# Splitting a mixer tile into front, ssm_front, scan and back, and emitting the next tile's front between scan and back

## The chip, the cores and the metric

The kernel runs on 8 cores of one Trainium2 chip. Every core works on its own prompt sequence and its own 16 sample sequences; no data goes between cores. The metric is the device time of the slowest core, in microseconds (us).

## The reference

One layer of a hybrid decoder, applied to a prompt (8 x 2048 x 1024) and to samples (128 x 4 x 1024):

```python
n1 = _rmsnorm(x, g_mix); proj = n1 @ w_in                  # 1024 -> 1536
u, v, xs = split(proj, [512, 1024])
v = _rmsnorm(v per head, g_v)
a_out = u * (tril(w_s[h]) @ v + b_s)                       # in chunks of 128 positions
ys, hr, hi = _ssm_scan(xs, h0_re, h0_im, ...)              # 32 groups, complex diagonal state of 64
g = gelu(ys); b_out = g * sigmoid(g @ w_glu + b_glu)
mix = concat(_rmsnorm(a_out), _rmsnorm(b_out))
h = x + mix @ w_out                                        # the residual addition
up = _rmsnorm(h) @ w_ffn_in; conv = causal conv of width 3 over up
y = _rmsnorm(h + (gelu(gate) * val) @ w_ffn_out)
```

The states of the scan, the last rows of up and, for the samples, v are outputs too.

## The kernel before

A core runs setup (tables and weights for the scan, to about 288 us in the profile), then the mixer, which makes h, then the FFN, which reads h back from a tensor h1d in device memory. A barrier over all engines stands between them. The change is in the mixer alone.

**How the program is ordered.** The kernel builds a list of instructions for each engine in the order in which the Python code emits them (class Prog). A Buf object stands for each buffer and keeps its last writer and its readers; an instruction waits on semaphores for the last writer of what it reads, and for the last writer and the readers of what it writes. On an engine the instructions stand in emission order. The DMAs issued by SP (called "sp") form one list with SP's waits, and those issued by POOL (the Z gathers) stand in POOL's list. Nothing reorders by hand or by a planner.

**A mixer tile** (mixer_tile, called five times: four prompt tiles of 512 tokens, then one sample tile of 64) handles subtiles s = 0 to 3 of 128 tokens, the sample tile only one of 64. Its parts, in emission order:

- The x loads: four DMAs of 512 KB into xt, a buffer of four subtiles. For the sample tile, also 32 small DMAs of the old states into Hin (in R1 and R2's memory) and their transposes.
- a2(s) and a4(s): Square of x with a sum (ACT), root (ACT), reciprocal (DVE, L328), xn = x * rs * g_mix (DVE), eight transposes (PE), copy into n1T (ACT).
- stage1(s): 24 projection matmuls with w_in. stage1e(s): copies of u and xs out of the PSUM banks (ACT), the store of xs to a scratch tensor zscr, and the gather of it into Z with another layout, by a DMA that POOL issues.
- stage2(s): RMSNorm of v, matmul with Msg, and a_tm = (s + b_s) * u (DVE). stage2b(s): RMSNorm of a_tm into mixa (DVE), transposes, copy into mixT (ACT). It runs one subtile behind stage2.
- ssm_front, emitted after stage2(3) and before stage2b(2): transposes of Z into X2, copied out by ACT and DVE, matmuls with MinX, and sixteen products of DVE into R1, R2, mA and mB, which POOL sums.
- The scan: 64 tensor_tensor_scan instructions of DVE (L783), and products that give HPb and the carries C1 and C2, with mB from POOL.
- The rest: 64 matmuls with Toep and Mout, copies into Z (DVE and ACT in turn), transposes, gelu into gT (ACT), a cast of gT to gTb (DVE), the GLU matmuls, sigmoid and product into mixT, Square into sqb, and w_out: per subtile 16 matmuls into four banks and four DVE instructions that add to xt, then the store of xt to h1d.

PSUM banks are taken in turn, eight of them, by nb(). L254 and L257 are the helpers of matmul and transpose, L260 and L276 those of ACT, L263, L272 and L278 those of DVE, L281 that of the DMAs. The last loop of ffn_tile is a part that the prediction also looks at: per subtile it loads h1d into hb (three buffers), has 44 matmuls, adds them to hb on DVE, normalises and stores hb to yp:

```python
for si, (hrow, PT, oap, col0) in enumerate(subtiles):
    i3 = cnt["hb"] % 3; cnt["hb"] += 1
    dma("sp", hb[i3][0:PT, :], h1d[hrow:hrow + PT, :], [], [b_hb[i3]])
...
    dma("sp", oap, hb[i3][0:PT, :], [b_hb[i3]], [], is_output=True)
```

Of the kernel before, what the change touches and what calls it, by code (L numbers as in the profile page):

```python
# [207 lines left out]
def build_nc():  # L208
# [28 lines left out]
    zscr = nc.dram_tensor("zscr", [2112, 512], BF16).ap()  # L237

    ES = contextlib.ExitStack()
    with ES:  # L240
# [267 lines left out]
        with contextlib.ExitStack() as SA:  # L508
# [21 lines left out]
            xt = sba("xt", [128, 4, 1024]); b_xts = [Buf() for _ in range(4)]  # L530
# [14 lines left out]
            mixT = sba("mixT", [128, 8, 512], BF16); b_mixT = Buf()  # L545
# [7 lines left out]
            gT = sba("gT", [128, 4, 512]); b_gT = Buf()  # L553
# [3 lines left out]
            bT = gT; b_bT = b_gT  # L557
# [36 lines left out]
            def mixer_tile(tok0, src, ntok, sample, h1row):  # L594
# [3 lines left out]
                if sample:  # L598
                    dma("sp", xt[0:64, 0, :], src, [], [b_xts[0]])
                else:  # L600
                    for s_ in range(4):
                        dma("sp", xt[:, s_, :], src[tok0 + 128 * s_:tok0 + 128 * (s_ + 1), :], [], [b_xts[s_]])
                if sample:
                    bk1, bbk1 = nb(); bk2, bbk2 = nb()
                    for gq in range(8):
                        gs = slice(gq * 4, gq * 4 + 4)
                        Hin = Hins[gq % 2]; b_Hin = b_Hins[gq % 2]
                        dma("sp", Hin[:, :, 0:64], sre[:, gs, :], [], [b_Hin]); dma("sp", Hin[:, :, 64:128], sim[:, gs, :], [], [b_Hin])
                        dma("sp", Hin[:, :, 128:192], sim[:, gs, :], [], [b_Hin]); dma("sp", Hin[:, :, 192:256], sre[:, gs, :], [], [b_Hin])
                        for gl in range(4):  # L610
                            g = gq * 4 + gl
                            tr(bk1[:, g * 16:(g + 1) * 16], Hin[:, gl, 0:128], identf[0:16, 0:16], [b_Hin, b_identf], [bbk1])
                            tr(bk2[:, g * 16:(g + 1) * 16], Hin[:, gl, 128:256], identf[0:16, 0:16], [b_Hin, b_identf], [bbk2])
                    f2 = lambda v_: v_.rearrange("p g b -> p (g b)")
                    cp("act", f2(V10), bk1[:, 0:512], [bbk1], [b_V10])
                    cp("dve", f2(V20), bk2[:, 0:512], [bbk2], [b_V20])
                    cp("dve", HPb[:, :, 0:16], V10, [b_V10], [b_HPb])
                    shb = [128, 32, 16]
                    tt("dve", Vend, V10, AR4[:].unsqueeze(2).broadcast_to(shb), ALU.mult, [b_V10, b_A4], [b_Vend])
                    tt("dve", Vt, V20, AI4[:].unsqueeze(2).broadcast_to(shb), ALU.mult, [b_V20, b_A4], [b_Vt])  # L620
                    tt("dve", Vend, Vend, Vt, ALU.add, [b_Vend, b_Vt], [b_Vend])

                b_ss_s = [Buf() for _ in range(4)]; b_rs_s = [Buf() for _ in range(4)]; b_tm_s = [Buf() for _ in range(4)]
                b_n1T_s = b_n1T_list

                def a2(s):
                    act(junk[0:PT, :], xt[0:PT, s, :], AF.Square, [b_xts[s]], [b_junk, b_ss_s[s]], accum_out=ss4[0:PT, s:s + 1])
                    rstd(rs4[0:PT, s:s + 1], ss4[0:PT, s:s + 1], 1024.0, PT, 1, [b_ss_s[s]], [b_rs_s[s]], tm4[0:PT, s:s + 1], b_tm_s[s])

                def a4(s):  # L630
                    k2 = s % 2
                    stt(xn[k2][0:PT, :], xt[0:PT, s, :], rs4[0:PT, s:s + 1], gmix_bc[0:PT, :], ALU.mult, ALU.mult,
                        [b_xts[s], b_rs_s[s], b_gmix], [b_xn[k2]])
                    bk, bb = nb()
                    bkb = bk[:].bitcast(BF16)
                    for dti in range(8):
                        tr(bkb[:, dti * PT:(dti + 1) * PT], xn[k2][0:PT, dti * 128:(dti + 1) * 128], identb[0:PT, 0:PT],
                           [b_xn[k2], b_identb], [bb])
                    cp("act", n1T[:, :, s * 128:s * 128 + PT], bkb[:, 0:8 * PT].rearrange("p (a t) -> p a t", a=8), [bb], [b_n1T_s[s]])
# [19 lines left out]
                def stage1e(s, bu, bbu, bx, bbx):
                    k2 = s % 2  # L660
                    cp("act", u_tm[k2][0:PT, :], bu[0:PT, :], [bbu], [b_u[k2]])
                    cp("act", xs_tm[0:PT, s, :], bx[0:PT, :], [bbx], [b_xs_s[s]])
                    b_zs = Buf()
                    if sample:
                        dma("sp", zscr[2048:2112, :], xs_tm[0:64, 0, :], [b_xs_s[0]], [b_zs])
                        zv = zscr[2048:2112, :].rearrange("(b t) c -> b t c", t=4)
                        dma("pool", Z[0:16, 0:4, :], zv, [b_zs], [b_Z_s[0]])
                        dma("pool", Z[0:16, 4:8, :], zv, [b_zs], [b_Z_s[0]])
                    else:
                        r0 = h1row + 128 * s  # L670
                        dma("sp", zscr[r0:r0 + 128, :], xs_tm[:, s, :], [b_xs_s[s]], [b_zs])
                        dma("pool", Z[16 * s:16 * s + 16, :, :], zscr[r0:r0 + 128, :].rearrange("(k i) c -> k i c", i=8), [b_zs], [b_Z_s[s]])

                def stage2(s, bv, bbv):
                    k2 = s % 2
                    tsl = slice(s * 128, s * 128 + PT)
                    act(vsq[0:PT, :], bv[0:PT, :], AF.Square, [bbv], [b_vsq])
                    P.op("dve", lambda e: e.reduce_sum(out=ssv[0:PT, :], in_=vsq[0:PT, :].rearrange("p (h d) -> p h d", h=4), axis=AX.X),
                         [b_vsq], [b_ssv])
                    rstd(rv[0:PT, :], ssv[0:PT, :], 128.0, PT, 4, [b_ssv], [b_rv], tmv[0:PT, :], b_tmv)  # L680
                    tt("dve", vtmp[0:PT, :].rearrange("p (h d) -> p h d", h=4), bv[0:PT, :].rearrange("p (h d) -> p h d", h=4),
                       rv[0:PT, :].unsqueeze(2).broadcast_to([PT, 4, 128]), ALU.mult, [bbv, b_rv], [b_vtmp])
                    if sample:
                        tt("dve", vnf[0:PT, :], vtmp[0:PT, :], gv_bc[0:PT, :], ALU.mult, [b_vtmp, b_gv], [b_vnf])
                        dma("sp", vs, vnf[0:PT, :], [b_vnf], [], is_output=True)
                        cp("dve", vn[k2][0:PT, :], vnf[0:PT, :], [b_vnf], [b_vn[k2]])
                    else:
                        tt("dve", vn[k2][0:PT, :], vtmp[0:PT, :], gv_bc[0:PT, :], ALU.mult, [b_vtmp, b_gv], [b_vn[k2]])
                    bs_, bbs = nb()
                    for h in range(4):  # L690
                        lhs = Msg_s[:, h, :] if sample else Msg[:, h, :]
                        mm(bs_[0:PT, h * 128:(h + 1) * 128], lhs, vn[k2][0:PT, h * 128:(h + 1) * 128], True, True,
                           [b_Msg, b_vn[k2]], [bbs])
                    bsb = bsT_s if sample else bsT
                    a_tm = a_tms[k2]; b_atm = b_atms[k2]
                    for h in range(4):
                        stt(a_tm[0:PT, h * 128:(h + 1) * 128], bs_[0:PT, h * 128:(h + 1) * 128], bsb[0:PT, h:h + 1],
                            u_tm[k2][0:PT, h * 128:(h + 1) * 128], ALU.add, ALU.mult, [bbs, b_col, b_u[k2]], [b_atm])
# [51 lines left out]
                for s in range(NS):  # L750
                    nxt = stage1(s + 1) if s + 1 < NS else None
                    stage2(s, pend[0], pend[1])
                    if s == NS - 1:
                        b1, bb1 = ssm_front()
# [372 lines left out]
```

How the kernel before makes its waits and increments, by code:

```python
            def run(ename, eng):  # L158
                waited = {}
                for o in self.ops[ename]:
                    for d in o.deps:
                        if d.kind == "c":
                            key = ("c", d.eng)
                            val = d.seq
                            sem = esem[d.eng]
                        else:
                            key = ("d", d.eng, d.dsem)
                            val = d.dval
                            sem = dsem[d.eng][d.dsem]
                        if waited.get(key, 0) >= val:
                            continue
                        waited[key] = val
                        eng.wait_ge(sem, val)
                    ins = o.emit(eng)
                    if o.kind == "c":
                        if o.marked:
                            ins.then_inc(esem[ename], 1)
                    else:
                        ins.then_inc(dsem[ename][o.dsem], 16)
                fin = {}
                for o in self.out_dmas:
                    if o.eng == ename:
                        fin[o.dsem] = max(fin.get(o.dsem, 0), o.dval)
                for s, v in fin.items():
                    eng.wait_ge(dsem[ename][s], v)
```

## Time and profile before

| | us |
|---|---|
| runs shown | 1723.48 and 1761.52, median 1742.5 |
| the profiled execution, its own time | 1719.03 |
| its span, on the profiled core (5) | 1717.5 |
| spans of the eight cores in it | 1706.6 to 1717.5 |
| PE, DVE, ACT, POOL busy | 858.1, 902.4, 552.9, 305.7 |

The profile shows one execution on its slowest core. Busy times are sums over the span. A row of the timeline gives the start of an instruction (or of a run of like ones), its length, engine, line, kind, what it writes and reads, how many, and in brackets how long the engine was idle before it and who released it. Times of rows are counted from the span's start.

### The profile page before, as it was taken

The numbers are of one execution on the slowest core, as the hardware profiler recorded it, in microseconds if no ns is written. First come the engines' busy times: TensorE is split into PE (matmuls) and PEld (weight loads), VectorE is DVE, ScalarE is ACT, GpSimd is POOL, SyncE is SP. The second block draws the span as 40 slices with busy tenths as digits, with TensorE's granted clock in tenths as the row PEclk, the third lists the DMA queues.
The fourth block names the chain that finished last, engine by engine and source line by source line (L and its number), as shares of the span: only waits on it lengthen the run. The fifth ranks groups of instructions, "written<-read, shape, count | busy, mean of one in ns | idle before, by whom it ended". The sixth has DMA issues, their size and how long they took to land.

```text
span 1717.5 us, 18591 instructions; the slowest of 8 cores (1706.6 to 1717.5 us)
## 1 busy us (share of the span) xinstructions
PE 858.1 (50%) x4925; PEld 440.4 (26%) x4925; DVE 902.4 (53%) x1638; ACT 552.9 (32%) x1359; POOL 305.7 (18%) x319
## 2 busy tenths in 40 slices
PE   0002100615542561553242525877869378888696
PEld 0002100313221231322122313333324133334243
DVE  0388720484356348436531204899942258888522
ACT  0200101313322230332210306565631277676411
POOL 1000002030021003002100010555530014444200
PEclk9997555857765785776575656999989779999898
DMA  5600001000200200020010063777753435555033
GB/s 75 83 6 0 2 25 57 22 4 22 86 16 1 98 22 4 26 83 16 1 60 8 15 110 95 80 91 86 82 75 99 132 70 56 53 54 55 7 115 99
DMA packets 138807, 89.70 MB, mean 52 GB/s; under 512 B 115943, under 2 KB 122159, under 8 KB 138447
## 3 DMA queue, kind: packets, MB, share of 16 engines
q0 software_dynamic: 99136, 36.84, 19.0%
q1 hardware_dynamic: 39567, 51.67, 9.6%
q8 instruction: 41, 0.67, 0.2%
q14 instruction: 63, 0.52, 0.1%
HBM read 102.45 MB, written 20.64 MB: 72 GB/s over the span
## 4 chain that ended last, share of the span: by engine, by line
DVE 25%; DMA 24%; PE 19%; issue 14%; ACT 13%; POOL 3%; SPq 1%; DVEq 1%; ACTq 0%; POOLq 0%
PE bank L254 15%; DMA wst<-w_ffn_in 6%; DMA hb<-h1d 4%; DVE acc L272 4%; PE bank L257 3%; DVE R L783 3%; ACT acc L260 2%; ACT junkB L260 2%; DMA w_in_sb<-w_in 2%; POOL zt L263 2%; DMA R<-sim 2%; DMA R<-w_s 1%; DVE hb L263 1%; DVE hb L272 1%; DMA xt<-xp 1%
## 5 line engine op out<-in xcount | busy, mean ns | idle before, releaser
L254 PE MATMUL bank<-n2T,wst 128*128 128x512 bf16 (+1 forms) x1760 | 345.2, 357 | 64.4 <-ACT acc L260 25.4
L254 PEld LDWEIGHTS bank<-n2T,wst 128*128 128x128 bf16 x1760 | 154.6, 101 | 254.8 <-issue 106.2
L272 DVE SCALAR_TENSOR_TENSOR acc<-upS,cw,acc 128x512 f32<-128x512 f32 (+1 forms) x264 | 178.3, 688 | 30.6 <-ACT hsv L276 15.5
L260 ACT ACTIVATE acc<-bank,cw 128x512 f32<-128x512 f32 (+1 forms) x220 | 156.0, 709 | 111.2 <-POOL zt L263 111.2
L254 PE MATMUL bank<-wfo,zt 128*128 128x512 bf16 (+1 forms) x748 | 166.0, 386 | 25.2 <-POOL zt L263 25.2
L263 POOL TENSOR_TENSOR zt<-acc,acc 128x512 bf16<-128x512 f32 (+1 forms) x110 | 122.5, 1114 | 207.5 <-ACT cst_s L276 118.1
L272 DVE SCALAR_TENSOR_TENSOR acc<-bank,cw,acc 128x511 f32<-128x511 f32 (+1 forms) x176 | 131.2, 746 | 10.8 <-ACT upS L276 1.3
L281 POOL DMA_DIRECT2D wst<-w_ffn_in x88 | 79.7, 906 | 190.5 <-DMA wst<-w_ffn_in 180.0
L254 PEld LDWEIGHTS bank<-wfo,zt 128*128 128x128 bf16 (+1 forms) x748 | 74.5, 100 | 116.3 <-issue 31.6
L254 PE MATMUL bank<-w_in_sb,n1T 128*128 128x512 bf16 (+1 forms) x408 | 98.2, 402 | 0.8 <-ACT n1T L276 0.8
L281 POOL DMA_DIRECT2D Z<-zscr x18 | 9.0, 503 | 491.4 <-DMA zscr<-xs_tm 489.1
L257 PE MATMUL bank<-identf,R 16*128 16x16 f32 (+3 forms) x104 | 15.4, 299 | 155.8 <-DMA R<-w_s 111.4
L260 ACT ACTIVATE junkB<-hb 128x1024 bf16<-128x1024 f32 (+1 forms) x34 | 35.7, 1051 | 167.5 <-DVE hb L263 159.6
L272 DVE SCALAR_TENSOR_TENSOR acc<-hsv,cw,acc 128x1 f32<-128x1 f32 (+1 forms) x176 | 75.1, 426 | 19.7 <-DVE acc L272 1.8
L263 DVE TENSOR_TENSOR hb<-hb,bank 128x512 f32<-128x512 f32 (+1 forms) x34 | 23.4, 688 | 108.1 <-DMA hb<-h1d 80.7
L254 PE MATMUL bank<-Mout,HPb 128*64 128x128 bf16 (+1 forms) x160 | 30.5, 270 | 92.7 <-DVE C L263 92.7
L254 PE MATMUL bank<-w_out_sb,mixT 128*128 128x512 bf16 (+1 forms) x272 | 68.6, 419 | 0.0
L260 ACT ACTIVATE acc<-acc 128x512 f32<-128x512 f32 (+1 forms) x110 | 61.2, 556 | 14.3 <-DVE acc L272 14.2
L276 ACT ACTIVATE upS<-bank 128x512 f32<-128x512 f32 (+1 forms) x132 | 62.3, 472 | 9.6 <-PE bank L254 9.5
L260 ACT ACTIVATE gTb<-xt 128x1024 bf16<-128x1024 f32 (+1 forms) x17 | 17.9, 1050 | 124.8 <-DMA xt<-xp 124.8
L257 PE MATMUL bank<-identb,xn 128*128 128x128 bf16 (+1 forms) x136 | 16.8, 302 | 82.3 <-DVE xn L272 82.3
L254 PEld LDWEIGHTS bank<-w_in_sb,n1T 128*128 128x128 bf16 (+1 forms) x408 | 42.1, 105 | 51.6 <-issue 11.3
(220 smaller groups left out, 1276.7 us busy)
## 6 DMA issues: line engine op xcount, KB each, us to landing
wst<-w_ffn_in POOLq DMA_DIRECT2D x88, 256.0 KB, 4.5
hb<-h1d SPq DMA_DIRECT2D x32, 512.0 KB
xt<-xp SPq DMA_DIRECT2D x16, 512.0 KB
h1d<-xt SPq DMA_DIRECT2D x16, 512.0 KB
yp<-hb SPq DMA_DIRECT2D x16, 512.0 KB
wfo<-w_ffn_out POOLq DMA_DIRECT2D x22, 256.0 KB, 4.8
w_in_sb<-w_in POOLq DMA_DIRECT2D x8, 256.0 KB, 4.5
w_out_sb<-w_out POOLq DMA_DIRECT2D x8, 256.0 KB, 4.0
```

Of the source, the lines that this page charges most:

```text
L254: P.op("pe", lambda e: e.matmul(out, lhsT, rhs, start=start, stop=stop), reads, writes)
L257: P.op("pe", lambda e: e.transpose(out, in_, ident), reads, writes)
L260: P.op("act", lambda e: e.activation(out=out, in_=in_, func=func, **kw), reads, writes)
L263: P.op(eng, lambda e: e.tensor_tensor(out=out, in0=in0, in1=in1, op=op), reads, writes)
L272: P.op("dve", lambda e: e.scalar_tensor_tensor(out=out, in0=in0, scalar=scalar, in1=in1, op0=op0, op1=op1), reads, writes)
L276: P.op(eng, lambda e: e.activation(out=out, in_=in_, func=AF.Copy), reads, writes)
L281: P.dma(q, lambda e: e.dma_start(out=out, in_=in_, **kw), reads, writes, is_output=is_output)
L783: P.op("dve", lambda e, RR=RR, g=g: e.tensor_tensor_scan(out=RR[:, g, :], data0=MG8[:, g:g + 1].broadcast_to([128, 64]), data1=RR[:, g, :] ...
```

## The change

mixer_tile no longer runs a tile but returns four functions, and the caller emits them in a new order:

```python
tiles[0][0]()
tiles[0][1]()
for t in range(5):
    tiles[t][2]()
    if t + 1 < 5:
        tiles[t + 1][0]()
    tiles[t][3]()
...
    if t + 1 < 5:
        tiles[t + 1][1]()
```

[0] is front (x loads, a2, a4, stage1, stage1e, stage2, stage2b), [1] is ssm_front (now with the Z gathers, and for the sample tile with the loads of the old states), [2] is scan, [3] is back. The outputs of the prompt's last state are emitted after back(3). With that go these edits:

- xt with four subtiles becomes xa, two buffers of one subtile each for the front, and xh, two buffers of one subtile each for back. back loads x again from device memory into xh.
- The x load of subtile s is emitted in a2(s), and not four at once.
- The gather of Z is emitted in ssm_front. All zscr stores and Z gathers go by one Buf, b_zscr, where each store had one of its own.
- mixT is split into mixTa (two buffers, by the tile's parity) and mixTb.
- gT and its cast to bf16 are gone; gelu writes gTb.

```diff
-            xt = sba("xt", [128, 4, 1024]); b_xts = [Buf() for _ in range(4)]
+            xa = [sba("xa%d" % i, [128, 1024]) for i in range(2)]; b_xa = [Buf(), Buf()]
+            xh = [sba("xh%d" % i, [128, 1024]) for i in range(2)]; b_xh = [Buf(), Buf()]
...
+                    def a2(s):
+                        xs_ = xa[s % 2]; bxs_ = b_xa[s % 2]
+                        if sample:
+                            dma("sp", xs_[0:64, :], src, [], [bxs_])
+                        else:
+                            dma("sp", xs_[:, :], src[tok0 + 128 * s:tok0 + 128 * (s + 1), :], [], [bxs_])
+                        act(junk[0:PT, :], xs_[0:PT, :], AF.Square, [bxs_], [b_junk, b_ss_s[s]], accum_out=ss4[0:PT, s:s + 1])
...
+                    a2(0)
+                    for s in range(NS):
+                        if s + 1 < NS:
+                            a2(s + 1)
+                        a4(s)
...
+                    pend = stage1(0)
+                    stage1e(0, *pend[2:])
+                    lag = None
+                    for s in range(NS):
+                        nxt = stage1(s + 1) if s + 1 < NS else None
+                        stage2(s, pend[0], pend[1])
+                        if lag is not None:
+                            stage2b(lag)
+                        if nxt is not None:
+                            stage1e(s + 1, *nxt[2:])
+                        lag = s
+                        pend = nxt
+                    stage2b(lag)
...
+                        for s_ in range(4):
+                            r0 = h1row + 128 * s_
+                            dma("pool", Z[16 * s_:16 * s_ + 16, :, :], zscr[r0:r0 + 128, :].rearrange("(k i) c -> k i c", i=8), [b_zscr], [b_Zs[s_]])
...
+                            act(gTb[:, cb, 0:ntok].rearrange("p (k j) -> p j k", j=NJ),
+                                bkb[:, o0:o0 + NJ * NC].rearrange("p (j k) -> p j k", j=NJ), AF.Gelu_apprx_tanh, [bb], [b_gTb])
...
-                cp("dve", gTb[:, :, 0:ntok], gT[:, :, 0:ntok], [b_gT], [b_gTb])
...
+                    for s in range(NS):
+                        tsl = slice(s * 128, s * 128 + PT)
+                        hi_ = cnt_a["xh"] % 2; cnt_a["xh"] += 1
+                        xh_ = xh[hi_]; bxh_ = b_xh[hi_]
+                        if sample:
+                            dma("sp", xh_[0:64, :], src, [], [bxh_])
+                        else:
+                            dma("sp", xh_[:, :], src[tok0 + 128 * s:tok0 + 128 * (s + 1), :], [], [bxh_])
...
+                            xsl = xh_[0:PT, nh * 512:(nh + 1) * 512]
+                            tt("dve", xsl, xsl, bka[0:PT, :], ALU.add, [bxh_, bba], [bxh_])
+                            stt(xsl, bkb_[0:PT, :], rb4[0:PT, s:s + 1], xsl, ALU.mult, ALU.add, [bxh_, bbb, b_rb4], [bxh_])
+                        if sample:
+                            dma("sp", h1d[h1row:h1row + 64, :], xh_[0:64, :], [bxh_], [])
+                        else:
+                            dma("sp", h1d[h1row + 128 * s:h1row + 128 * (s + 1), :], xh_[:, :], [bxh_], [])
```

## Rows read from the trace of the kernel before

**Rows 1.** The profile's page, its head.

```profile
span 1717.5 us, 18591 instructions; the slowest of 8 cores (1706.6 to 1717.5 us)
```

**Rows 2.** Busy time by stretch: start and end, length, each engine, PEclk, DMA share, GB/s.

```profile
587.80:610.00 22.20, 3.79 (x32) 3.11 (x33) 5.70 (x8) 8.43 (x15) 0.00 (x0) 0.51 0.34 117
...
666.00:690.00 24.00, 0.83 (x5) 0.48 (x5) 22.72 (x90) 0.83 (x2) 5.04 (x4) 0.50 0.00 0
```

**Rows 3.** Timeline (columns as told above) of the start of tile 2.

```profile
586.11 0.75 DVE L272 SCALAR_TENSOR_TENSOR xt<-bank,rb,xt 128x512 f32<-128x512 f32 x1 [0.17 <-PE bank L254]
...
587.76 2.99 SPq L281 DMA_DIRECT2D xt<-xp  x4
...
592.16 1.06 ACT L260 ACTIVATE gTb<-xt 128x1024 bf16<-128x1024 f32 x1 [20.82 <-DMA xt<-xp]
...
593.79 0.16 DVE L328 RECIPROCAL rs<-tm 128x1 f32<-128x1 f32 x1 [6.93 <-ACT tm L260]
...
596.04 1.28 DVE L272 SCALAR_TENSOR_TENSOR xn<-xt,rs,gmix_bc 128x1024 bf16<-128x1024 f32 x1
...
606.62 2.48 DVE L272 SCALAR_TENSOR_TENSOR xn<-xt,rs,gmix_bc 128x1024 bf16<-128x1024 f32 x2
...
610.05 11.50 PE L254 MATMUL bank<-w_in_sb,n1T 128*128 128x512 bf16 x48
```

**Rows 4.** Timeline, the start of tile 0.

```profile
288.26 1.77 SPq L281 DMA_DIRECT2D xt<-xp  x4
...
291.97 1.06 ACT L260 ACTIVATE gTb<-xt 128x1024 bf16<-128x1024 f32 x1 [62.62 <-DMA xt<-xp]
```

**Rows 5.** Timeline of tile 2, from stage2(3) to the first Mout matmul.

```profile
646.11 1.71 DVE L272 SCALAR_TENSOR_TENSOR a_tm<-bank,bsT,u_tm 128x128 f32<-128x128 f32 x4 [0.84 <-PE bank L254]
...
649.54 0.69 DVE L278 COPY X<-bank 128x1024 bf16<-128x1024 bf16 x1 [1.72 <-ACT X L276]
...
661.46 0.77 DVE L272 SCALAR_TENSOR_TENSOR mixa<-a_tm,ra,goa_bc 128x512 bf16<-128x512 f32 x1
...
661.64 1.71 POOL L263 TENSOR_TENSOR R<-R,mB 128x512 f32<-128x512 f32 x1
...
666.04 0.58 PE L257 MATMUL bank<-identb,mixa 128*128 128x128 bf16 x4 [3.08 <-DVE cA L263]
...
666.63 5.56 DVE L783 TENSOR_TENSOR_SCAN R<-MG,R 128x64 f32<-128x64 f32 x24
...
690.04 0.28 PE L254 MATMUL bank<-Mout,HPb 128*64 128x128 bf16 x1 [23.18 <-DVE C L263]
```

**Rows 6.** Timeline of tile 2, gelu to GLU.

```profile
704.22 1.23 DVE L278 CAST gTb<-gT 128x2048 bf16<-128x2048 f32 x1 [7.66 <-ACT gT L260]
...
705.59 6.28 PE L254 MATMUL bank<-gTb,w_glu_sb 128*128 128x512 bf16 x16 [7.00 <-DVE gTb L278]
```

**Rows 7.** Timeline of tile 2, DVE's additions of w_out.

```profile
720.15 0.69 DVE L263 TENSOR_TENSOR xt<-xt,bank 128x512 f32<-128x512 f32 x1 [0.28 <-issue]
...
724.09 0.69 DVE L263 TENSOR_TENSOR xt<-xt,bank 128x512 f32<-128x512 f32 x1
...
733.64 0.75 DVE L272 SCALAR_TENSOR_TENSOR xt<-bank,rb,xt 128x512 f32<-128x512 f32 x1 [0.17 <-PE bank L254]
```

**Rows 8.** The FFN's h1d loads: who waited for them (us, times), then timeline rows.

```profile
  DVE hb L263: 80.7, 15
...
1291.10 0.69 DVE L263 TENSOR_TENSOR hb<-hb,bank 128x512 f32<-128x512 f32 x1 [7.13 <-DMA hb<-h1d]
...
1641.61 0.33 SPq L281 DMA_DIRECT2D hb<-h1d  x1
...
1645.68 0.69 DVE L263 TENSOR_TENSOR hb<-hb,bank 128x512 f32<-128x512 f32 x1 [4.63 <-DMA hb<-h1d]
```

**Rows 9.** Timeline of the sample tile, DVE and PE.

```profile
935.66 1.28 DVE L272 SCALAR_TENSOR_TENSOR xn<-xt,rs,gmix_bc 64x1024 bf16<-64x1024 f32 x1
...
959.49 5.64 PE L257 MATMUL bank<-identf,R 128*16 128x128 f32 x32 [0.54 <-ACT mixT L276]
```

More of the change, by code:

```diff
@@ L237, in build_nc @@
     zscr = nc.dram_tensor("zscr", [2112, 512], BF16).ap()
+    b_zscr = Buf()
     ES = contextlib.ExitStack()
@@ L597, in mixer_tile @@
                 NC = 16 if sample else 64
[L598 to L639, printed above, removed]
@@ L659, in stage1e @@
[L659 to L663, printed above, removed]
-                    if sample:
-                        dma("sp", zscr[2048:2112, :], xs_tm[0:64, 0, :], [b_xs_s[0]], [b_zs])
+                mixTa_t = mixTa[par]; b_mixTa_t = b_mixTa[par]
+                shared = {}
@@ L674, in stage2 @@
[L674 to L698, printed above, removed]
@@ L744, in ssm_front @@
                             tt("pool", R2[:, gs, :], R2[:, gs, :], mB[:], ALU.subtract, wr2 + [b_mB], wr2)
-                    return (b1, bb1) if sample else (None, None)
-                pend = stage1(0)
-                stage1e(0, *pend[2:])
-                lag = None
[L750 to L754, printed above, removed]
-                    if lag is not None:
-                        stage2b(lag)
-                    if nxt is not None:
-                        stage1e(s + 1, *nxt[2:])
-                    lag = s
-                    pend = nxt
@@ L765, in mixer_tile, with back @@
+                def back():
+                    Zy = Z
                     for gq in range(8):
@@ L829, in mixer_tile @@
-                act(sqb[:, :, 0:ntok], mixT[:, 4:8, 0:ntok], AF.Square, [b_mixT], [b_sqb, b_R1[8]])
-                bkR, bbR = nb()
-                for s in range(NS):
-                    tsl = slice(s * 128, s * 128 + PT)
-                    for m in range(4):
-                        mm(bkR[0:PT, s:s + 1], sqb[:, m, tsl], onesb[:, 0:1], m == 0, m == 3, [b_ones, b_sqb, b_R1[8]], [bbR])
-                rstd(rb4[0:PT, 0:NS], bkR[0:PT, 0:NS], 512.0, PT, NS, [bbR], [b_rb4], tb4[0:PT, 0:NS], b_tb4)
@@ L849, in mixer_tile @@
-                if sample:
-                    dma("sp", h1d[h1row:h1row + 64, :], xt[0:64, 0, :], [b_xts[0]], [])
-            for t in range(4):
-                mixer_tile(512 * t, xp, 512, False, 512 * t)
-            bk, bb = nb()
-            tr(bk[0:32, 0:128], C1[:], identf[:], [b_C, b_identf], [bb])
-            cp("act", stS[:], bk[0:32, 0:128], [bb], [b_stS])
-            dma("sp", srep, stS[:, 0:64], [b_stS], [], is_output=True)
-            dma("sp", simp, stS[:, 64:128], [b_stS], [], is_output=True)
@@ L859, in build_nc @@
-            mixer_tile(0, xs, 64, True, 2048)
+                            if sample:
+                                mm(bk[0:NC, gl * 128:(gl + 1) * 128], X2[0:64, g, 0:NC], Toep[0:64, g, :], True, False, [b_X2, b_Toep], [bb])
+                            else:
+                                mm(bk[0:NC, gl * 128:(gl + 1) * 128], X2[:, g, 0:NC], Toep[:, g, :], True, False, [b_X2, b_Toep], [bb])
+                            mm(bk[0:NC, gl * 128:(gl + 1) * 128], HPb[:, g, 0:NC], Mout[:, g, :], False, True, [b_HPb, b_Mout], [bb])
@@ new lines, in back @@
+                        cp("dve" if gq % 2 == 0 else "act", Zy[0:NC, :, 64 * gq:64 * gq + 64].rearrange("p j (g c) -> p g j c", g=4),
+                           bk[0:NC, 0:512].rearrange("p (g j c) -> p g j c", g=4, j=8), [bb], b_Zs)
+                    NJ = 4 if sample else 8
+                    for cbp in range(2):
+                        bk, bb = nb()
+                        bkb = bk[:].bitcast(BF16)
+                        for cl in range(2):
+                            cb = cbp * 2 + cl
+                            for j in range(NJ):
+                                o0 = (cl * NJ + j) * NC
+                                tr(bkb[:, o0:o0 + NC], Zy[0:NC, j, cb * 128:(cb + 1) * 128], identb[0:NC, 0:NC], b_Zs + [b_identb], [bb])
+                        for cl in range(2):
+                            cb = cbp * 2 + cl
+                            o0 = cl * NJ * NC
+                            act(gTb[:, cb, 0:ntok].rearrange("p (k j) -> p j k", j=NJ),
+                                bkb[:, o0:o0 + NJ * NC].rearrange("p (j k) -> p j k", j=NJ), AF.Gelu_apprx_tanh, [bb], [b_gTb])
@@ new lines, in back @@
+                    for m in range(4):
+                        bk, bb = nb()
+                        for kt in range(4):
+                            mm(bk[:, 0:ntok], w_glu_sb[:, kt, m * 128:(m + 1) * 128], gTb[:, kt, 0:ntok], kt == 0, kt == 3, [b_wglu, b_gTb], [bb])
+                        act(sg[:, 0:ntok], bk[:, 0:ntok], AF.Sigmoid, [bb, b_col], [b_sg], bias=bglu[:, m:m + 1])
+                        tt("dve", mixTb[:, m, 0:ntok], gTb[:, m, 0:ntok], sg[:, 0:ntok], ALU.mult, [b_gTb, b_sg], [b_mixTb])
@@ new lines, in back @@
+                    act(sqb[:, :, 0:ntok], mixTb[:, :, 0:ntok], AF.Square, [b_mixTb], [b_sqb, b_R1[8]])
+                    bkR, bbR = nb()
+                    for s in range(NS):
+                        tsl = slice(s * 128, s * 128 + PT)
+                        for m in range(4):
+                            mm(bkR[0:PT, s:s + 1], sqb[:, m, tsl], onesb[:, 0:1], m == 0, m == 3, [b_ones, b_sqb, b_R1[8]], [bbR])
+                    rstd(rb4[0:PT, 0:NS], bkR[0:PT, 0:NS], 512.0, PT, NS, [bbR], [b_rb4], tb4[0:PT, 0:NS], b_tb4)
@@ new lines, in mixer_tile @@
+                return front, ssm_front, scan, back
+            tiles = [mixer_tile(512 * t, xp, 512, False, 512 * t, t % 2) for t in range(4)]
+            tiles.append(mixer_tile(0, xs, 64, True, 2048, 0))
+            tiles[0][0]()
[5 more added lines that the diff above has]
+                tiles[t][3]()
+                if t == 3:
+                    bk, bb = nb()
+                    tr(bk[0:32, 0:128], C1[:], identf[:], [b_C, b_identf], [bb])
+                    cp("act", stS[:], bk[0:32, 0:128], [bb], [b_stS])
+                    dma("sp", srep, stS[:, 0:64], [b_stS], [], is_output=True)
+                    dma("sp", simp, stS[:, 64:128], [b_stS], [], is_output=True)
+                if t + 1 < 5:
+                    tiles[t + 1][1]()
```

252 lines of the change are left out of this document (140 added, 112 removed).

## The prediction

> **What bounds the kernel now.** I read the page first: the profiled core spans 1717.5 us [rows 1], and outside that span the execution's own time of 1719.0 us has 1.5 us. The part that is changed, the mixer, runs from the first x load at 288.3 us [rows 4] to the barrier ahead of the FFN. No engine is full there, so I cut one prompt tile (tile 2) into stretches and looked in each for the wait that ends last. Three things stand out.
>
> At the tile's start everything stands still for x. DVE ends the previous tile's last addition at 586.86, SP issues the four x loads at 587.76, ACT gets the first at 592.16, and the first projection matmul runs at 610.05, 23.2 us after DVE's last work [rows 3]. Most of that is not the load: it is a ring Square, reciprocal, xn, transposes, copy, repeated for each subtile, with PE busy 3.79 us of 22.2 [rows 2].
>
> In the scan DVE is busy 22.72 of 24 us and PE 0.83 [rows 2]; PE's first Mout matmul has then waited 23.18 us for DVE [rows 5]. So the scan is DVE's, and the scan is the bound there.
>
> Last, w_out: PE and DVE alternate, 3.94 us for subtile 0 and (734.39 - 724.09) / 3 = 3.43 us for each of the others [rows 7]. x is in SBUF then, nothing waits for a DMA.
>
> **The change part by part.** The emission order becomes scan(t), front(t+1), back(t), ssm_front(t+1). Each engine still runs its own list in order. The row of mixa(2) shows it: DVE ran it at 661.46 with no idle time before it, straight after the sixteen products that stand ahead of it in the list [rows 5]. So what counts is what each engine has ahead of the moved work.
>
> *Front under the scan.* Every subtile of the front needs DVE (reciprocal and xn) before PE can transpose. These stand behind scan(t) on DVE. Only the loads, Squares and roots of subtiles 0 and 1 can run under the scan, on SP and ACT. PE's idle 23 us stay.
>
> *The x ring.* xt held four subtiles, xa holds two. Loads 0 and 1 of tile t+1 stand on SP behind back(t-1)'s last store and land under ssm_front(t) and scan(t): hidden. Load 2 needs xa[0], read by xn(0), which DVE runs after scan(t); load 3 needs xa[1], read by xn(1), which stands behind reciprocal 2, which needs load 2. Both loads are exposed, one after the other. A load issued into a quiet queue took 291.97 - 288.26 = 3.7 us until ACT ran [rows 4]; Square to reciprocal is 593.79 - 592.16 = 1.6; xn is 1.3 (half of 2.48); from xn(2)'s start to the first matmul 610.05 - 606.62 = 3.4 [rows 3]. From scan end: reciprocals and xn(0) 1.7, load 3.7, Square path 1.6, reciprocal and xn(1) 1.5, load 3.7, Square path 1.6, reciprocal 0.2, 3.4: 17.4, with 0.1 for each of some six handovers 18.0 us. Before it was 23.2. Saved 5.2 for tiles 1 to 3: -15.6. Tile 0 has no earlier work to hide under: xn(0) to matmul was 610.05 - 596.04 = 14.0 [rows 3], becomes 18.0 - 0.4 = 17.6: +3.6.
>
> *Stage 2 to scan.* ssm_front stood between stage2(3) and stage2b(2), so that products and mixa shared the time: a_tm ended at 647.8 (four of 1.71 us in all from 646.11) and the scan began at 666.63, 18.8 us [rows 5]. Now both stage2b come first: from mixa(2) (661.46) to the end of PE's transposes of mixa(3) (666.04 + 0.58) is 5.2, with 0.4 for the reciprocal 5.6 us, and PE turns to back(t). ssm_front then stands alone, from the X copy (649.54) to POOL's last sum (661.64 + 1.71 = 663.35) and 0.6 for the carries: 14.4 us [rows 5]. 5.6 + 14.4 = 20.0 against 18.8: +1.2 for each of four tiles, +4.8. The Z gathers move on POOL's queue from the front to ssm_front. They need back(t)'s transposes of Z, done before the GLU, and POOL has nothing else; w_out covers them at no cost, otherwise one gather after another of a few us would be late, then the X transposes. The shared b_zscr chains the zscr stores; SP waits there, but xh load 0 behind it is wanted only 30 us later.
>
> *gT goes.* The cast of 1.23 us and its handovers go: PE began the GLU 705.59 - 704.22 = 1.4 us after the cast's start [rows 6]; -1.4 each, -5.5 for four tiles.
>
> *The residual is loaded again.* back loads x a second time. In SP's list this is load(s), store(s), load(s+1), store(s+1). Store(s) waits for DVE's last addition of s, and load(s+1) stands behind it, although xh has another buffer that is free. So load(s+1) is issued when DVE has run dry, and DVE waits for all of it; 3 per tile, 12 in all (load 0 and the sample's lie ahead of other work). Behind DVE's waiting addition stand the rest of back and all of ssm_front(t+1): its X copy is a DVE instruction, so the scan is late by the same. The kernel has the same pattern with the same 512 KB in its FFN: hb load behind the yp store. There DVE waited 80.7 us over 15 times, 5.4 each; from 4.63 (a load issued at 1641.61) to 7.13 [rows 8]. I take the mean. The additions, now free of PE, run 0.1 faster than 3.43. 12 x (5.4 - 0.1) = +63.6.
>
> *Sample tile.* Its front goes from between the state loads and the state output (935.66 to 959.49 [rows 9]) to between scan(3) and back(3). About as long in either place, and nothing runs beside it in either: I cost this at 0, bounds -3 and +3. The state loads keep their chain.
>
> Sum: 3.6 - 15.6 + 4.8 - 5.5 + 63.6 = +50.9. 1719.0 + 50.9 = 1770 us. The two runs shown are 1723.5 and 1761.5, median 1742.5; the profiled execution is 0.3% under the lower one, and my time is to be held against executions like it. A median like theirs would stand some 20 us higher.
>
> Of the load's price: the rows say 3.9 to 7.1 us for 512 KB. The Trainium skill, DMA: Bandwidth & Descriptors, section on the anatomy of one DMA, gives about 2.0 us fixed plus bytes over bandwidth (for DMAs issued from GpSimd), and its Bandwidth section about 358 GB/s per core where both cores of a pair stream; an estimate by that page is 3.5 us, and the sum with it would be near 1756. The trace's loads are longer than that page's figure, so it is not used.
>
> **The rivals.**
>
> *The second load is covered (the other side, not slower).* Were the 12 loads to land under DVE's additions, the sum would be 50.9 - 63.6 = -12.7, 1706 us. It turns where a load costs 12.7 / 12 = 1.1 us; a result within 2% of before needs less than (34.4 + 12.7) / 12 = 3.9. For it: two xh buffers, and PE, done ahead by two subtiles, never waits. Against: SP's order, and the 15 waits of hb, which has three buffers and waits nevertheless. Chance 0.08. The Trainium skill, same page, Rules for kernel authors, says to issue a DMA early, compute, and wait late, since the fixed cost then overlaps. By that rule this would be the result, if the issue were early; the rows of hb show what a store ahead in the queue makes of it.
>
> *The change does what its name says.* The front truly runs under the scan: 3 x 18.0 us less than my sum, 1716 us. For it: PE and ACT are free. Against: xn is DVE's. Chance 0.03.
>
> *The stores get in the way.* Each xh load runs beside the store issued 0.5 us earlier, as hb's do. At the dearest wait, 7.13, the sum is 12 x 1.7 = 21 higher, 1791; if loads 2 and 3 of x also take the 4.4 us of the first load of tile 2, issued behind a store (592.16 - 587.76 [rows 3]), in place of 3.7, it is 8 x 0.7 = 6 more: 1797. Chance 0.17.
>
> *Cheap end.* Every load at 4.63: 12 x 0.8 = 9 less, 1761; with 3 us from the sample tile, and 0.6 per tile if PE, fresh from the front, ran the first four GLU matmuls at the pace of w_in's (11.50 / 48 = 0.24 [rows 3] against 6.28 / 16 = 0.39 [rows 6]), 1756. Chance 0.2, and the forecast itself 0.52.
>
> **How the numbers follow.** The range 1750 to 1806 takes in the forecast, the cheap end and the store case, with 6 to 9 us beyond for what I rounded and, above, for a median that like the one shown lies over the profiled execution; left out are the first two rivals, 0.11, and the tails. About 2%, 34 us, is what a measurement can tell from no change; slower by over that begins at 1753 in this accounting. The forecast, the cheap end (nearly all) and the dear end lie past it: 0.76. Within 2%: the two first rivals and the rest of the cheap end, 0.2. Faster by over 2% needs the front hidden and the loads hidden: 0.04.
>
> **What would show it.** Right: DVE waits for xh<-x some 5 us twelve times, each behind an h1d store; the gap of PE before the first Mout matmul stays; ACT waits for x twice per tile, about 3 us, after xn(0) and xn(1); a steady tile lasts 147.5 - 5.2 + 1.2 - 1.4 + 15.9 = 158 us, where 147.5 is the distance between DVE's last additions of two tiles, 586.86 and 734.39 [rows 3, 7]. Wrong: xh waits under 2 us; or PE transposes xn during the scan. The weakest term is the price of one exposed load; 1 us there is 12 us in the sum.

## The result and the profile after

| | before | changed | 
|---|---|---|
| median of all runs, us | 1729.6 (10 runs) | 1793.0 (11 runs) |
| the profiled execution, us | 1719.0 | 1784.2 |

The changed kernel is slower: the ratio of its time to that of before is 1.0366, with a 95% interval of 1.0335 to 1.0396. The forecast was 1770, made against 1719; the profiled executions differ by 65.1 us where the sum had 50.9. Some executions of every kernel fall into a slower state with a lower TensorE clock: the medians here are of all executions and the ratios of the others alone, and of the profiles used below only that of the old order with the new buffers shows such an execution. The page of the changed kernel begins:

```profile
span 1782.6 us, 18661 instructions; the slowest of 8 cores (1772.1 to 1782.6 us)
...
PE 863.9 (48%) x4925; PEld 439.9 (25%) x4925; DVE 902.5 (51%) x1633; ACT 575.5 (32%) x1359; POOL 303.3 (17%) x319
...
DVE  0398711483256426432822011688982238888632
```

DVE's busy time has not moved (902.5 against 902.4), PE's has grown by 6 us and ACT's by 22.6 (575.5 against 552.9), the span [rows 1] by 65. Over the whole span no engine is full: most of the 65 us is time in which engines wait for one another, and the third point below shows what ACT's 22.6 us are.

The first thing to look at is the start of tile 2, the timeline of the same stretch as [rows 3], DVE first, then ACT and PE (start, length, what, and in brackets the idle time before and its releaser; the helpers' lines stand one lower than in the kernel before, L261 for L260, L273 for L272 and so on):

```profile
559.52 0.17 DVE L264 TENSOR_TENSOR C<-cA,cB 128x8 f32<-128x8 f32 x1
...
559.89 1.28 DVE L273 SCALAR_TENSOR_TENSOR xn<-xa,rs,gmix_bc 128x1024 bf16<-128x1024 f32 x1
...
566.58 0.16 DVE L329 RECIPROCAL rs<-tm 128x1 f32<-128x1 f32 x1 [5.40 <-ACT tm L261]
...
564.94 1.06 ACT L261 ACTIVATE gTb<-xa 128x1024 bf16<-128x1024 f32 x1 [1.48 <-DMA xa<-xp]
...
571.95 1.06 ACT L261 ACTIVATE gTb<-xa 128x1024 bf16<-128x1024 f32 x1 [1.64 <-DMA xa<-xp]
...
561.32 1.01 PE L258 MATMUL bank<-identb,xn 128*128 128x128 bf16 x8 [34.94 <-DVE xn L273]
...
577.26 11.71 PE L255 MATMUL bank<-w_in_sb,n1T 128*128 128x512 bf16 x48
```

The scan ends at 559.69, and xn(0) follows with no gap: loads 0 and 1 are hidden. ACT waits for loads 2 and 3, DVE for ACT, and w_in's matmuls begin 17.6 us after the scan's end, where it was 23.2 after DVE's last addition. PE has waited 34.94 us for xn: nothing of the front was under the scan except what SP and ACT had of it.

Second, the additions of w_out, SP's list and DVE's (compare [rows 7, 8]), and then, from the view of the tile xh, what the instructions that write it waited for in the whole execution (us, times):

```profile
661.32 0.32 SPq L282 DMA_DIRECT2D h1d<-xh  x1
...
661.78 0.33 SPq L282 DMA_DIRECT2D xh<-xp  x1
...
665.84 0.69 DVE L264 TENSOR_TENSOR xh<-xh,bank 128x512 f32<-128x512 f32 x1 [4.60 <-DMA xh<-xp]
...
675.55 0.69 DVE L264 TENSOR_TENSOR xh<-xh,bank 128x512 f32<-128x512 f32 x1 [6.32 <-DMA xh<-xp]
...
687.22 0.68 DVE L279 COPY X<-bank 128x1024 bf16<-128x1024 bf16 x1
```

```profile
  DMA xh<-xp: 55.0, 11
```

Store, load, wait, as in the FFN. Eleven waits are put down to the load, 5.0 us each, and the additions of a tile take 29.9 us (657.38 to 687.30) in place of 14.2. The X copy of the next ssm_front stands right behind them at 687.22. The prediction had twelve such waits.

Third, what was not forecast, gelu and the GLU's first matmul (compare [rows 6]), first in the kernel before and then in the changed one:

```profile
699.50 4.62 ACT L260 ACTIVATE gT<-bank 128x512 f32<-128x512 bf16 x4
```

```profile
632.75 10.00 ACT L261 ACTIVATE gTb<-bank 128x512 bf16<-128x512 bf16 x4
...
643.00 6.02 PE L255 MATMUL bank<-gTb,w_glu_sb 128*128 128x512 bf16 x16 [10.78 <-ACT gTb L261]
```

The four gelu instructions of a tile take 10.0 us; in the kernel before they took 4.6. PE waits 10.78 us for them, where it waited 7.00 for gelu and the cast [rows 6].

### The profile page after: what moved, and what is told of

Same layout as the page of the kernel before. It is cut to its first block, busy times and chain, and to the rows that moved or that the text cites. A ratio compares the mean times of both kernels' runs of the same rounds, so it can differ in the third digit from the quotient of the medians.

```text
span 1782.6 us, 18661 instructions; the slowest of 8 cores (1772.1 to 1782.6 us)
## 1 busy us (share of the span) xinstructions
PE 863.9 (48%) x4925; PEld 439.9 (25%) x4925; DVE 902.5 (51%) x1633; ACT 575.5 (32%) x1359; POOL 303.3 (17%) x319
## 4 chain that ended last, share of the span: by engine, by line
DVE 28%; DMA 24%; PE 16%; ACT 13%; issue 13%; POOL 3%; SPq 1%; DVEq 1%; ACTq 0%; POOLq 0%
PE bank L255 14%; DMA wst<-w_ffn_in 6%; DVE acc L273 5%; DMA hb<-h1d 4%; ACT gTb L261 3%; DVE R L793 3%; DMA xh<-xp 2%; PE bank L258 2%; ACT acc L261 2%; DMA xa<-xp 2%; ACT junkB L261 2%; DMA w_in_sb<-w_in 2%; POOL zt L264 2%; DMA R<-sim 1%; DVE hb L264 1%
## 5 line engine op out<-in xcount | busy, mean ns | idle before, releaser
L273 DVE SCALAR_TENSOR_TENSOR acc<-upS,cw,acc 128x512 f32<-128x512 f32 (+1 forms) x264 | 178.9, 691 | 36.8 <-ACT hsv L277 22.1
L261 ACT ACTIVATE acc<-bank,cw 128x512 f32<-128x512 f32 (+1 forms) x220 | 155.9, 709 | 113.2 <-POOL zt L264 113.2
L273 DVE SCALAR_TENSOR_TENSOR acc<-bank,cw,acc 128x511 f32<-128x511 f32 (+1 forms) x176 | 131.2, 745 | 10.7 <-ACT upS L277 1.6
L258 PE MATMUL bank<-identb,xn 128*128 128x128 bf16 (+1 forms) x136 | 16.8, 301 | 194.9 <-DVE xn L273 194.9
L255 PE MATMUL bank<-w_in_sb,n1T 128*128 128x512 bf16 (+1 forms) x408 | 102.6, 415 | 0.8 <-ACT n1T L277 0.8
L261 ACT ACTIVATE junkB<-hb 128x1024 bf16<-128x1024 f32 (+1 forms) x34 | 35.8, 1052 | 161.3 <-DVE hb L264 152.5
L273 DVE SCALAR_TENSOR_TENSOR acc<-hsv,cw,acc 128x1 f32<-128x1 f32 (+1 forms) x176 | 76.7, 436 | 18.3
L277 ACT ACTIVATE n1T<-bank 128x1024 bf16<-128x1024 bf16 (+1 forms) x17 | 17.0, 998 | 160.1 <-PE bank L258 160.1
L261 ACT ACTIVATE acc<-acc 128x512 f32<-128x512 f32 (+1 forms) x110 | 61.2, 556 | 13.0 <-DVE acc L273 12.9
L258 PEld LDWEIGHTS bank<-identb,xn 128*128 128x128 bf16 (+1 forms) x136 | 12.8, 136 | 198.4 <-issue 198.4
L264 DVE TENSOR_TENSOR xh<-xh,bank 128x512 f32<-128x512 f32 (+1 forms) x34 | 23.4, 687 | 67.3 <-DMA xh<-xp 55.0
L264 DVE TENSOR_TENSOR mixTb<-gTb,sg 128x512 bf16<-128x512 bf16 (+1 forms) x20 | 12.0, 599 | 89.7 <-ACT sg L261 89.7
```

Source lines behind the costliest of these rows:

```text
L255: P.op("pe", lambda e: e.matmul(out, lhsT, rhs, start=start, stop=stop), reads, writes)
L258: P.op("pe", lambda e: e.transpose(out, in_, ident), reads, writes)
L261: P.op("act", lambda e: e.activation(out=out, in_=in_, func=func, **kw), reads, writes)
L264: P.op(eng, lambda e: e.tensor_tensor(out=out, in0=in0, in1=in1, op=op), reads, writes)
L273: P.op("dve", lambda e: e.scalar_tensor_tensor(out=out, in0=in0, scalar=scalar, in1=in1, op0=op0, op1=op1), reads, writes)
L277: P.op(eng, lambda e: e.activation(out=out, in_=in_, func=AF.Copy), reads, writes)
```

## The experiments

All times are medians; the kernel before stood at 1728.6 to 1730.1 beside them. The changed kernel was not run again beside them: its time is the 1793.0 of the result above.

**Gelu to f32 again.** The changed kernel, with gelu's output in R2's memory, which is free in back:

```diff
+            gT = R2[:].rearrange("p g k -> p (g k)").rearrange("p (a t) -> p a t", a=4)
...
-                            act(gTb[:, cb, 0:ntok].rearrange("p (k j) -> p j k", j=NJ),
+                            act(gT[:, cb, 0:ntok].rearrange("p (k j) -> p j k", j=NJ),
...
+                    cp("dve", gTb[:, :, 0:ntok], gT[:, :, 0:ntok], b_R2, [b_gTb])
```

> The changed kernel with gelu written to f32 again (into R2's memory, which is free in back) and cast to bf16, as in the kernel before; all else as changed. Theory A, the strided bf16 output is what makes gelu slow (four of them 10.0 us in the changed kernel, 4.6 before): gelu falls to 4.6 us, from the table load to the first GLU matmul it is 7.4 us again in place of 11.6, and the time falls by 4 x 4.2 = 17 us, to 1776 from a median of 1793. Rival B, gelu is slow for another reason that came with the new order (what ran before it, the banks, the power state): gelu stays at 10 us, the cast comes on top, +5 us, 1798.

Measured: 1773.1, ratio to before 1.0245 (1.0207 to 1.0283), 20 us under the changed kernel. The groups of gelu by form, of the kernel before, the changed kernel and this one (busy us in all, mean ns of one; idle time before):

```profile
L260 ACT ACTIVATE gT<-bank 128x512 f32<-128x512 bf16 x16 | 17.4, 1085 | 1.4 <-ACT gT L260 0.4
```

```profile
L261 ACT ACTIVATE gTb<-bank 128x512 bf16<-128x512 bf16 x16 | 38.9, 2431 | 1.1
```

```profile
L261 ACT ACTIVATE R<-bank 128x512 f32<-128x512 bf16 x16 | 17.4, 1085 | 1.1
```

2431 ns become 1085 again, the kernel before's own figure, with all else in the new order. Theory A, that gelu's output is the cause, holds (it expected 1776).

**The same edit alone, in the kernel before.**

```diff
-                        act(gT[:, cb, 0:ntok].rearrange("p (k j) -> p j k", j=NJ),
+                        act(gTb[:, cb, 0:ntok].rearrange("p (k j) -> p j k", j=NJ),
...
-                cp("dve", gTb[:, :, 0:ntok], gT[:, :, 0:ntok], [b_gT], [b_gTb])
```

> The kernel before with one edit of the change alone: gelu writes bf16 straight into gTb and the cast is gone. Theory A, strided bf16 output is slow in any place: gelu 10 us in place of 4.6, less the cast, +4.2 per prompt tile, +17, 1747 from 1730. Rival B, as the prediction had it: the cast's 1.4 us go and nothing else changes, -5.5, 1724.

Measured: 1741.4, ratio 1.0071 (1.0052 to 1.0089). The same group by form:

```profile
L260 ACT ACTIVATE gTb<-bank 128x512 bf16<-128x512 bf16 x16 | 38.9, 2432 | 1.4 <-ACT gTb L260 0.4
```

2432 ns in the old order too. The edit costs 13 us by the medians and 19 by the profiled executions (1737.9 against 1719.0), on either side of the 17 expected; a step that I had counted as a gain is a loss in both orders.

**Gelu in plain order.** The changed kernel, with the two rearranges of gelu gone:

```diff
-                            act(gTb[:, cb, 0:ntok].rearrange("p (k j) -> p j k", j=NJ),
-                                bkb[:, o0:o0 + NJ * NC].rearrange("p (j k) -> p j k", j=NJ), AF.Gelu_apprx_tanh, [bb], [b_gTb])
+                            act(gTb[:, cb, 0:ntok],
+                                bkb[:, o0:o0 + NJ * NC], AF.Gelu_apprx_tanh, [bb], [b_gTb])
```

> The changed kernel with gelu reading its bank and writing gTb in plain order, both contiguous, still bf16; this leaves out the reordering of tokens, so y is another. Theory A, the slow gelu comes of writing two-byte values at a stride of eight: contiguous, one takes 0.6 to 1.1 us in place of 2.43, and the time is 20 us or more under the changed kernel. Rival B, it comes of bf16 output from this bank as such: 2.4 us as before the edit, no gain.

Measured once: 1756.6, 36 us under the changed kernel. The same group:

```profile
L261 ACT ACTIVATE gTb<-bank 128x512 bf16<-128x512 bf16 x16 | 9.6, 597 | 1.1
```

597 ns. So bf16 as such is not slow. The input was read in the same order in all of them; what differs is the output's step: none, 597 ns; eight f32 elements (32 bytes), 1085; eight bf16 elements (16 bytes), 2431. The Trainium skill, SBUF — State Buffer, in its note on cachelines in the section on the DMA port swizzle, says that SBUF has lines of 16 bytes and that each access to a new line costs extra. Both strided outputs take a new line for each element, so the rule agrees with both being slower than 597, but it doesn't say why 16-byte steps of bf16 are 2.2 times as dear as 32-byte steps of f32.

The sample tile's gelu is a second case, with a step of four elements in place of eight. From the same views, the changed kernel, the kernel before and this one:

```profile
L261 ACT ACTIVATE gTb<-bank 128x64 bf16<-128x64 bf16 x4 | 1.2, 310 | 0.3
```

```profile
L260 ACT ACTIVATE gT<-bank 128x64 f32<-128x64 bf16 x4 | 1.1, 282 | 0.3
```

```profile
L261 ACT ACTIVATE gTb<-bank 128x64 bf16<-128x64 bf16 x4 | 0.9, 224 | 0.3
```

Here the strided bf16 output is only 1.1 times as dear as the f32 one (310 against 282 ns; contiguous 224). So the price of a strided bf16 output depends on the step and not on the type alone, and lines of 16 bytes don't account for it: at this step bf16 has two elements to a line and f32 one, and bf16 is still the dearer. The cause stays open.

**The residual loads early.** Four xh buffers don't fit into SBUF, the on-chip memory, beside the rest (gTb then needs 4096 bytes per partition where 3200 are left). So in the changed kernel subtiles 0 and 3 go into xh, 1 and 2 into R2's memory, and no load stands behind a store:

```diff
+                    xhs = [(xh[0], [b_xh[0]]), (R2v[:, 0:1024], b_R2[0:16]), (R2v[:, 1024:2048], b_R2[16:32]), (xh[1], [b_xh[1]])]
...
+                    xload(0)
+                    if not sample:
+                        xload(3)
                     for gq in range(8):
...
+                    if not sample:
+                        xload(1)
+                        xload(2)
                     act(sqb[:, :, 0:ntok], mixTb[:, :, 0:ntok], AF.Square, [b_mixTb], [b_sqb, b_R1[8]])
...
-                        hi_ = cnt_a["xh"] % 2; cnt_a["xh"] += 1
-                        xh_ = xh[hi_]; bxh_ = b_xh[hi_]
+                        xh_, bxh_ = xhs[s]
```

> The changed kernel with the four residual loads of a tile issued early: the first and last subtile into xh at the start of back, the two in the middle into R2's memory (free in back) after the GLU; no load stands behind a store any more. Theory A, the exposed residual loads are the main loss: the 11 waits of DVE for xh in the profiled execution (55 us) and a twelfth go, and the time falls by 55 to 60 from a median of 1793, to 1735. By the runs so far the two repairs together gave 1717 and gelu alone 20 of it, so 1736 again. Rival B, the two losses overlapped in part, and each repair alone gives more than its share: 1728 or less, or the loads alone give less, 1745 or more.

Measured: 1737.3, ratio 1.0047 (1.0028 to 1.0067), 56 us under the changed kernel. SP's list in tile 2, and then what the instructions that write xh still wait for:

```profile
597.80 0.88 SPq L282 DMA_DIRECT2D xh<-xp  x2
...
598.88 1.49 SPq L282 DMA_DIRECT2D R<-xp  x2
...
647.92 0.33 SPq L282 DMA_DIRECT2D h1d<-xh  x1
```

```profile
  PE bank L255: 11.7, 24
```

The loads go out 49 us ahead of the first store; no wait for xh<-xp or for R<-xp is left, only PE's pace. 56 is the whole of the 55.0 that DVE had waited.

**Both repairs.** The edits of gelu to f32 and of the early loads together, in the changed kernel. While gelu uses R2's memory, the two residual loads that go there wait until the product with the GLU's gate has read it.

> The two repairs together, f32 gelu with cast (its own run: 1773) and early residual loads; the new order stays. Theory A, the two losses lie one behind the other on the same chain and add: 1793 - 20 - 57 = 1716, 0.7% under before (1729), which is what the hidden x loads of the new order are worth less the longer way to the scan (-12.7 in the prediction's sum). Rival B, the order is worth more once nothing hides it: 1700 or less. Rival C, it costs: over before, 1735 or more. In this kernel gelu's output and two of the loads share R2, so loads 1 and 2 are issued only some 5 us ahead of the additions; up to 2 us a tile may be exposed.

Measured: 1716.6, ratio 0.9917 (0.9888 to 0.9945). The two losses add (20 + 56 = 76, measured 1793.0 - 1716.6 = 76.4). With them gone, the rest of the change is 13 us faster than the kernel before (1730.1 beside it). The prediction's terms without the loads and without gelu come to 3.6 - 15.6 + 4.8 = -7.2; the profiled executions, by which the sum was made, give -7.4 (1711.66 against 1719.03), and the medians -13.4. Where the 6 us between the two come from isn't shown: the profiled execution of the kernel before is faster than each of its executions beside this one (1726.6 to 1738.0).

**The old order, with the new buffers.** The loop at the end of the mixer:

```diff
                 tiles[t][2]()
-                if t + 1 < 5:
-                    tiles[t + 1][0]()
                 tiles[t][3]()
...
                 if t + 1 < 5:
+                    tiles[t + 1][0]()
                     tiles[t + 1][1]()
```

> The changed kernel with the emission order undone (scan, back, then front and ssm_front of the next tile), all buffers as changed. Theory A, the new order is worth the x loads 0 and 1 and their Squares, nothing more: without it from scan or back to the first projection matmul about 26.4 us in place of 17.6, 3 x 8.8 for the prompt tiles and some 4 for the sample tile, +30, 1823. Rival B, the new order is worth nothing or costs (front ahead of back delays back and no engine gains): 1793 or less. Rival C, the front did hide behind more than that: 1850 or more.

Measured: 1820.1, ratio 1.0510 (1.0469 to 1.0551), 27 us over the changed kernel. So the new order of the tiles by itself brings 27 us, and what comes with it (the buffers, gelu's output, ssm_front behind stage2b) costs 90: 76 are the two losses, and the other 14 were not taken apart. With two x buffers the old order has no load of x under a scan at all. Its profile shows what that costs in tile 1, DVE's last addition of tile 0 and then PE:

```profile
457.77 0.75 DVE L273 SCALAR_TENSOR_TENSOR xh<-bank,rb,xh 128x512 f32<-128x512 f32 x1 [0.17 <-DVE xh L264]
...
484.37 11.65 PE L255 MATMUL bank<-w_in_sb,n1T 128*128 128x512 bf16 x48
```

That is 25.9 us, against 17.7 in the changed kernel and 23.0 in the kernel before; in tiles 2 and 3 it is 24.6 and 24.7. So three prompt tiles make up some 23 of the 27; the rest wasn't looked for.

**The front really between the scan's instructions.** front and scan become generators that yield at some points, and the caller takes them in turn. On top of both repairs:

```diff
+                        a4(s)
+                        yield "a4"
...
+                        if s == 0:
+                            yield "s1"
                         stage2(s, pend[0], pend[1])
...
+            SCHED = (1, 15, 31, 32, 33)
             for t in range(5):
-                tiles[t][2]()
-                if t + 1 < 5:
-                    tiles[t + 1][0]()
+                fr_ = tiles[t + 1][0]() if t + 1 < 5 else iter(())
+                n_ = 0
+                for _ in tiles[t][2]():
+                    n_ += 1
+                    if n_ in SCHED:
+                        next(fr_, None)
+                for _ in fr_:
+                    pass
                 tiles[t][3]()
```

scan yields after each pair of scan instructions (32 times) and after each quarter of the closing products.

> The kernel of the two repairs, with the front of tile t+1 emitted in pieces between the instructions of scan(t): a2 and a4 of subtile 0 after the first pair of scan instructions, subtile 1 after 15 pairs, 2 and 3 near pair 32, and stage1(0), its copies and stage1(1) after the first quarter of the closing products. The rest of the front follows the scan. Theory A, DVE's order alone kept the front from running beside the scan: now x's ring (17.6 us) and the first two subtiles' 48 matmuls (11.7) run beside the scan, against 6 us of DVE's time put into it: 23 us less for each of three prompt tiles and some 8 for the sample's, 1716 - 77 = 1640. Rival B, the front is bound by its own chain and DVE's inserted instructions wait on loads and stop the scan: 1700 or more.

Measured: 1646.0, ratio 0.9501 (0.9463 to 0.9540): 5.0% under the kernel before and 71 us under the kernel of the two repairs. DVE in tile 1's scan, then PE beside it:

```profile
494.62 0.48 DVE L797 TENSOR_TENSOR_SCAN R<-MG,R 128x64 f32<-128x64 f32 x2
...
495.26 1.28 DVE L273 SCALAR_TENSOR_TENSOR xn<-xa,rs,gmix_bc 128x1024 bf16<-128x1024 f32 x1
...
496.46 6.27 DVE L797 TENSOR_TENSOR_SCAN R<-MG,R 128x64 f32<-128x64 f32 x28
...
502.71 1.26 DVE L273 SCALAR_TENSOR_TENSOR xn<-xa,rs,gmix_bc 128x1024 bf16<-128x1024 f32 x1
...
522.32 0.68 DVE L264 TENSOR_TENSOR HPb<-mA,mB 128x504 bf16<-128x504 f32 x1 [0.17 <-DVE mA L264]
...
513.99 11.08 PE L255 MATMUL bank<-w_in_sb,n1T 128*128 128x512 bf16 x47 [0.22 <-issue]
```

xn(0) and xn(1) stand between scan instructions with no idle time, and the projection matmuls of the next tile start at 513.99, before the last HPb product at 522.32. Busy times of a whole scan (start and end, length, PE, PEld, DVE, ACT, POOL, granted clock, DMA share, GB/s), first of the changed kernel, then of this one:

```profile
535.00:560.00 25.00, 0.00 (x0) 0.00 (x0) 23.36 (x94) 0.00 (x0) 5.21 (x5) 0.50 0.00 1
```

```profile
494.00:524.00 30.00, 14.05 (x75) 7.73 (x77) 28.75 (x100) 8.66 (x13) 5.29 (x5) 0.64 0.12 40
```

PE goes from 0 to 14.05 us of work, and DVE stays full. The scan is 5 us longer and takes in 5 us of DVE's own front work.

**The interleaving without the repairs.** The edit of the last kernel alone, in the changed kernel: gelu writes bf16, and the residual loads stand behind the stores.

> The changed kernel with the pieces of the next front put between the instructions of the scan, and neither repair: gelu slow, residual loads behind the stores. Theory A, DVE's list is what kept the front from hiding, and its worth is independent of the two losses: 70 less, as between the kernels with the repairs (1717 to 1646), 1793 - 70 = 1723, about the time before. Rival B, a hidden front needs the repairs (DVE idles for loads in back, so the DVE time put into the scan is paid twice, or x's loads come late): 1745 or more.

Measured: 1718.3, ratio 0.9934 (0.9912 to 0.9955), 75 us under the changed kernel. A holds: hiding the front under the scan is worth about the same with and without the two losses, which are both still there (twelve waits for xh, 60.2 us in all, and gelu at 2432 ns), and by itself makes up for both.

## Why the prediction was right, and which term was mis-sized

The direction, the range and the main mechanism held; one term had the wrong sign. That 1784 lies in the upper half of the range is in part luck: that half was there for dearer loads, the loads came out a little cheaper, and what filled it was gelu, for which the range had no allowance. The working, term by term, with the measured size as the difference of the two profiled executions over all tiles:

| step | forecast, us | measured, us |
|---|---|---|
| x ring, tiles 1 to 3 | -15.6 | -16.8 |
| x ring, tile 0 | +3.6 | +3.0 |
| first w_in matmul to the last a_tm | 0 | +3.6 |
| stage2b, ssm_front and scan | +4.8 | +3.1 |
| first Z copy to the first GLU matmul (gelu, cast) | -5.5 | +16.4 |
| GLU to the first addition | 0 | +0.3 |
| additions with exposed loads | +63.6 | +62.6 |
| sample tile | 0 | -2.6 |
| outside the mixer | 0 | -4.5 |
| sum | +50.9 | +65.1 |

- **Front under the scan:** right. DVE's order holds the front back; PE waits 34.94 us for xn in the changed kernel, and putting pieces of the front between the scan's instructions, and nothing else, took 75 us off.
- **The x ring:** right within 2 us; 17.7, 17.6 and 17.2 us from scan end to w_in against the 18.0 worked out. Load 2 took the 3.7 us of the sum (issued at 561.26, ACT began at 564.94). ACT's idle waits for it and for load 3 were 1.5 and 1.6 us and not the 3 named as a sign, as ACT copied n1T in the meantime.
- **The residual loads:** right, and the largest term. It came out a little lower (5.0 a wait against 5.4), and its removal gave 56 us.
- **"gT goes":** the step that failed, as "-1.4 each, -5.5 for four tiles". I took the cast's 1.23 us away and left gelu at its length in f32, though the edit changes what gelu writes: two-byte values at a step of eight. The term is 22 us off, and the experiments give it in both orders: 20 us in the changed kernel, 13 in the kernel before. The prediction had no row for a strided bf16 output of ACT and no bound for it either, where it bounded every load.
- **Stage 1:** 3.6 us that I had at 0. In tile 2 the fourth subtile's w_in matmuls take 8.10 us in place of 5.34, at a granted clock of 0.66 in that stretch against 1.00 in the kernel before, so in part at 1.2 GHz instead of 2.4 (first the changed kernel's timeline, then that of before):

```profile
597.97 8.10 PE L255 MATMUL bank<-w_in_sb,n1T 128*128 128x512 bf16 x24
```

```profile
630.46 5.34 PE L254 MATMUL bank<-w_in_sb,n1T 128*128 128x512 bf16 x24
```

  One of four tiles shows it that strongly. In the kernel of both repairs the fourth subtile's matmuls take 6.8 us in every tile, at a granted clock of 0.78, and the stage lasts 7.5 us longer than before over the four tiles (160.5 against 153.0). So the new order pays back a part of its gain here; no run separates why the clock is lower.
- **The rivals:** "the second load is covered" is what the early-loads kernel is. It is 8 us over the kernel before and not 12.7 under it, since gelu stays slow; with gelu repaired as well it is 13.4 under by the medians and 7.4 by the profiled executions. "The change does what its name says" had 1716, 3 under the kernel before, for the hidden front; the interleaved kernel without repairs is 11 under by the medians and 1 over by the profiled executions. It hides more than the x ring, the first 48 matmuls too, and pays in gelu.
- **Two figures of the prediction** don't come out. The sum by the page's 3.5 us a load is 1770 - 12 x (5.4 - 3.5) = 1747, not 1756. And the chance of 0.76 for slower by over 2% isn't the sum of its parts: 0.52, 0.17 and nearly all of 0.2 make some 0.87.

What stays open is the outer 4.5 us (setup is 3.2 us shorter, the FFN 1.3), code that the change doesn't touch.

## What to carry to other kernels

Moving a piece of work ahead of another in the emission hides it only on the engines whose lists are free: if each step needs one instruction of the busy engine, it has to be put between that engine's instructions, not behind them. A load emitted after a store that waits for compute, in the same list, is not a prefetch, however many buffers there are. And when an edit changes the type or the step of an output, its instruction has to be priced anew; the cast that it saves can be the cheaper way.

## What the runs showed of the hardware that was not expected

ACT's gelu on 128x512 from a PSUM bank took 597 ns with contiguous bf16 output, 1085 ns with f32 at a step of eight elements, and 2431 ns with bf16 at a step of eight elements, in the old order and the new alike. At that step the narrower type is 2.2 times as slow. At a step of four elements, in the sample tile's 128x64, it was 1.1 times (310 against 282 ns).
